# A fused two-block layer on one core: another order of the first loads, the first products and the first norm

## The reference

```python
def rmsnorm(x, g):
    xf = x.astype(jnp.float32)
    y = xf * lax.rsqrt(jnp.mean(xf * xf, axis=-1, keepdims=True) + EPS)
    return (y * g.astype(jnp.float32)).astype(x.dtype)

def gated_branch_mixer(h, w_in, ...):
    proj = h @ w_in                       # 1024 x 6144
    a_val, a_gate, u_pool, c_x, c_b, c_c, g = jnp.split(proj, PROJ_SPLITS, axis=-1)
    a = a_val * jax.nn.sigmoid(a_gate)
    a = causal_dwconv(a, conv_a_w) + conv_a_b
    ...

def first_block(x, mem, ...):
    h = rmsnorm(x, norm_mix_g[l])
    x = x + gated_branch_mixer(h, w_in[l], ...)
    x = x + memory_cross_attention(...)
    x = x + hierarchical_moe(...)
    return rmsnorm(x, norm_f_g)
```

## Time and profile before

| | us |
|---|---|
| median of 3 runs | 988.87 (988.23 to 990.27) |
| span of the profiled execution | 986.0 |
| what lies around the span, against the median | 2.9 |
| PE busy | 968.0 (98%) |
| first product | 5.89 |
| first split product (half chunk 4) | 23.62 |

### The profile page before, as it was taken

How to read it: one execution, slowest core, us unless ns; L and a number is a source line. 1 busy time by engine, 2 the same in 40 slices (tenths; PEclk the granted TensorE clock), 3 DMA queues, 4 the chain that set the end, 5 groups by cost and what they waited for, 6 DMA issues and landing times.

```text
span 986.0 us, 16667 instructions
## 1 busy us (share of the span) xinstructions
PE 968.0 (98%) x6553; PEld 888.3 (90%) x6553; DVE 749.4 (76%) x1135; ACT 518.2 (53%) x752; POOL 40.5 (4%) x42
## 2 busy tenths in 40 slices
PE   7999999999999999999999999999999999999997
PEld 6999998999999888888889999887999998999996
DVE  5699878679776886878867877965476289787876
ACT  4545533534453675777754545445465465555544
POOL 0002001000101000000001000000100120000000
PEclk9999999999999999999999999999999999999999
DMA  7945643446540677978873534221543255555541
GB/s 280 350 158 176 209 168 128 171 171 214 171 145 1 219 258 266 329 264 296 319 268 109 176 110 164 63 67 64 192 169 132 86 191 188 195 181 196 180 169 43
DMA packets 49601, 178.39 MB, mean 181 GB/s; under 512 B 5632, under 2 KB 5888, under 8 KB 49280
## 3 DMA queue, kind: packets, MB, share of 16 engines
q1 hardware_dynamic: 47952, 172.51, 51.0%
q10 hardware_dynamic: 1584, 4.99, 1.4%
HBM read 176.43 MB, written 1.05 MB: 180 GB/s over the span
## 4 chain that ended last, share of the span: by engine, by line
PE 91%; DVE 6%; DMA 1%; ACT 1%; issue 1%; DVEq 0%; SPq 0%; ACTq 0%
PE psum L715 90%; DVE wl L2169 2%; DVE work L2169 1%; DMA raw<-stream_in 1%; DVE xl L2207 1%; PE psum L953 1%; PE psum L1258 0%; DVE work L2994 0%; DVE xh L2202 0%; DVE rstd L2197 0%; DVE xT L2169 0%; ACT wh L1671 0%; DVE work L3057 0%; DVE ypair L2169 0%; ACT work L1598 0%
## 5 line engine op out<-in xcount | busy, mean ns | idle before, releaser
L1671 ACT CAST wh<-raw 128x1024 fp32r<-128x1024 f32 x292 | 303.5, 1050 | 285.3 <-PE psum L715 247.4
L2169 DVE TENSOR_TENSOR wl<-raw,wh 128x1024 fp32r<-128x1024 f32 x292 | 349.2, 1228 | 72.4 <-ACT wh L1671 69.5
L715 PE MATMUL psum<-xh,wh 128*128 128x256 f32 x976 | 275.6, 282 | 2.6 <-DVE wl L2169 2.0
L715 PE MATMUL psum<-xl,wh 128*128 128x256 f32 x976 | 272.6, 279 | 0.0
L715 PE MATMUL psum<-xh,wl 128*128 128x256 f32 x976 | 272.1, 279 | 0.0
L715 PEld LDWEIGHTS psum<-xh,wh 128*128 128x128 f32 x976 | 183.4, 188 | 5.9 <-issue 2.5
L715 PEld LDWEIGHTS psum<-xl,wh 128*128 128x128 f32 x976 | 183.5, 188 | 0.5
L715 PEld LDWEIGHTS psum<-xh,wl 128*128 128x128 f32 x976 | 183.4, 188 | 0.0
L715 PE MATMUL psum<-wh,slots 128*128 128x512 f32 x320 | 101.6, 391 | 0.0
L715 PE MATMUL psum<-memn,raw 128*128 128x256 f32 x320 | 73.3, 382 | 0.0
L715 PE MATMUL psum<-yh,wh 128*128 128x256 f32 x256 | 71.9, 281 | 0.3 <-DVE wl L2169 0.3
(11 more groups left out here) (276 smaller groups left out, 1484.9 us busy)
## 6 DMA issues: line engine op xcount, KB each, us to landing
raw<-stream_in SPq DMA_DIRECT2D x325, 512.0 KB, 4.5
memn<-mem_t_in ACTq DMA_DIRECT2D x2, 1024.0 KB, 8.6
out_rows<-work SPq DMA_DIRECT2D x4, 256.0 KB, 2.2
const<-const_in ACTq DMA_DIRECT2D x1, 581.0 KB, 3.6
xT<-x_t_in SPq DMA_DIRECT2D x2, 256.0 KB, 4.7
xT<-x_t_in ACTq DMA_DIRECT2D x2, 256.0 KB, 5.5
raw<-stream_in SPq DMA_DIRECT2D x2, 256.0 KB, 5.5
mask<-mask_in ACTq DMA_DIRECT2D x1, 512.0 KB, 13.7
```

The source lines that it names most:

```text
L715: return nc.tensor.matmul(out, w, x, start=start, stop=stop, **kw)
L1671: nc.scalar.copy(wh[:, SLOT[c], :], raw[:, c % RAW, :]).then_inc(hi_ready, 1)
L2169: return v.tensor_tensor(out, a, b, op)
```

## The change

SP now loads the four pairs of tiles of x, then half chunks 2 to 5. ACT loads, after the gains, half chunks 0 and 1 in four parts; part m has from both half chunks the 256 columns that belong to tiles 2m and 2m+1, so each transfer has two runs of 1 KB in every partition. `project_native` for unit 0 is replaced by `first_chunk`, which takes for each pair m the products of half chunks 0 and 1 and then the sum of squares of that pair. Nine products of zeros (128x512, bfloat16) stand ahead on PE. On ACT the root stands ahead of the rounding of half chunk 4. On DVE the subtraction for half chunk 4 stands ahead of the four that make `xl`, and PE's first split unit waits for `xh`, `xl` by pairs of tiles.

```diff
@@ sync: loads
-            for m in range(2):
-                q, w = slice(2 * m, 2 * m + 2), slice(HW // 2 * m, HW // 2 * (m + 1))
+            for m in range(4):
+                q = slice(2 * m, 2 * m + 2)
                 sp.dma_start(xT[:, q, :], xt_in[:, q, :]).then_inc(s_x[m], 16)
-                sp.dma_start(raw[:, 0, w], stream[0][:, w]).then_inc((s_first, landed[0])[m], 16)
-            for c in range(1, RAW):
+            for c in range(2, RAW):
                 load(c)
@@ tensor
-            def columns(out, slot, x):
+            def columns(out, slot, x, tile_pairs=None):
                 for k in range(DK):
+                    if tile_pairs and k % 2 == 0:
+                        pe.wait_ge(tile_pairs, k // 2 + 1)
...
+            def first_chunk():
+                u = units.take()
+                for m in range(4):
+                    pe.wait_ge(first_part[m], 16)
+                    for j in range(2):
+                        for k in (2 * m, 2 * m + 1):
+                            if j == 0:
+                                pe.wait_ge(xg_ready, k + 1)
+                            last = matmul(psum[:, u, j * T:(j + 1) * T], raw[:, j, k * P:(k + 1) * P], xg32[:, k, :],
+                                          k == 0 and j == 0, k == DK - 1, skip_group_check=True)
+                        if m == 3:
+                            last.then_inc(half_done, 1)
+                    pe.wait_ge(sq_folded, m + 1)
+                    last = matmul(psum[:, STAT, 0:T], ones, sq[:, 2 * m, :], m == 0, m == 3)
+                last.then_inc(stats_done, 1)
...
+            pe.wait_ge(zeroed, 2)
+            for _ in range(9):
+                matmul(psum[:, 6, :], zeros[:], zeros[:, 0:1].to_broadcast([P, 512]), True, True)
             pe.wait_ge(ones_set, 1)
-            project_native(C_WIN, xg32, xg_ready, lambda: stats(0))
+            first_chunk()
             project_native(C_WIN + 1, xg32)
-            pe.wait_ge(xn_ready, 4)
-            for n in range(C_WIN + 2, C_WIN + 16):
+            project(C_WIN + 2, xg, xn_ready)
+            for n in range(C_WIN + 3, C_WIN + 16):
                 project(n, xg)
@@ scalar
-            for m in (2, 3):
-                act.dma_start(xT[:, 2 * m:2 * m + 2, :], xt_in[:, 2 * m:2 * m + 2, :]).then_inc(s_x[m], 16)
+            for m in range(4):
+                w = slice(256 * m, 256 * (m + 1))
+                act.dma_start(raw[:, 0:2, w], stream[0:2, :, w].rearrange("h p w -> p h w")).then_inc(first_part[m], 16)
...
+            root(0)
             high.upto(4)
-            root(0)
@@ vector
                 tt(xn[:, q, :], xg32[:, q, :], two(rstd[:, 0, :]), ALU.mult).then_inc(xn_made, 1)
+            rest.upto(4)
             for m in range(4):
                 q = slice(2 * m, 2 * m + 2)
                 dve.wait_ge(xn_hi, m + 1)
```

More of the change, by code:

```diff
@@ L437, in build @@
         s_x = [sem(f"x_loaded{m}") for m in range(4)]
-        s_first = sem("first_half_chunk_loaded")
+        s_first = [sem(f"first_chunk_part{m}_loaded") for m in range(2)]
         s_mem = sem("mem_loaded")
@@ L446, in build @@
         low_ready = sem("low_ready")
+        first_part = (*s_first, landed[0], landed[1])
         half_done = sem("half_done")
@@ L741, in columns, with project @@
                 return last
-            def project(n, x):
+            def project(n, x, tile_pairs=None):
                 u = units.take()
@@ L749, in project @@
                     wait_split(c)
-                    columns(psum[:, u % UNITS, j * T:(j + 1) * T], SLOT[c], x).then_inc(half_done, 1)
+                    columns(psum[:, u % UNITS, j * T:(j + 1) * T], SLOT[c], x, None if j else tile_pairs).then_inc(half_done, 1)
             def project_rows(n, x):
@@ L998, in _, with project_native @@
             xg, yg = (xh, xl), (yh, yl)
-            def project_native(n, x, tile_ready=None, between=None):
+            def project_native(n, x):
                 u = units.take()
@@ L1005, in project_native @@
                     c = 2 * n + j
[L1006 to L1009, removed]
+                    wait_raw(c)
                     for k in range(DK):
[L1011 to L1014, removed]
                         last = matmul(psum[:, u % UNITS, j * T:(j + 1) * T], raw[:, c % RAW, k * P:(k + 1) * P],
@@ L1017, in project_native @@
                     last.then_inc(half_done, 1)
-                    if between and j == 0:
-                        between()
+            def first_chunk():
[13 more added lines that the diff above has]
+                last.then_inc(stats_done, 1)
             def native_rows(n, x, u):
```

## The result

The changed kernel is slower: 992.67 us, median of 7 runs (989.74 to 994.77), against 988.87 for the kernel before; ratio 1.0035, 95% interval 1.0024 to 1.0045. That is 3.4 us (2.4 to 4.5). The profiled execution has a span of 988.8 us against 986.0, 2.8 more; it took 990.60 us, 2.1 less than the median, so it is one of the quicker ones.

What follows compares the result with a forecast made beforehand. PE was taken as the bound (busy 968.0 of 986.0 us), the total following half chunk 6's start. Root 18.0 plus 13.7 gives 31.7 against 29.38, +2.3; 988.9 + 2.3 = 991.2 us, range 988.0 to 993.3.

Steps and rivals of the forecast that it cites:

- chain behind the root: Dependent work from root to `wl` of half chunk 6 stays 13.6 us; half chunk 6 starts 13.7 us after the root.
- main line: Late parts put the root at 18.0 and half chunk 6 at 31.7 against 29.38: +2.3 us; higher clock for all pairs.
- PE idle before pairs 1 and 2: Sign of the forecast at the head: PE waits for late parts, with pauses of 0.6 and 1.3 us.
- Rival A: Head loads: turns go by whole transfers, parts keep pace with x, root 15.4, total 988.6; chance 0.13.
- second limit: Root to `wl` of half chunk 6, before the change: 13.6 us of dependent work with only 1.0 us to spare.
- 1 KB price: Time one DMA engine spends on a 1 KB piece of ACT's parts: taken as 50 ns, between 45 and 53.
- sum of turns: Head loads: engines alternate single pieces of SP's and ACT's queues, so parts 0 to 3 land at 7.0, 9.8, 13.2, 15.3.
- 4 KB price: Time one DMA engine spends on a 4 KB piece of SP's half chunks: 161 ns.
- The clock: PE at the head: zeros from about 1.0 to 4.9 us raise the clock to the higher level (2.4 GHz) for all pairs.
- rival B: Head: parts late and PE's clock low for one pair or more, root +0.4 to +1.4, middle 992.2 us; chance 0.25.
- Stiff block: PE's work behind the head moves as one block: the total moves by what the start of half chunk 6 moves.

Runs made afterwards that it cites:

- after_again: The changed kernel measured once more with no edit: 992.40 us, ratio 1.0027 to the kernel before.
- no_zeros: The changed kernel without the nine products of zeros: 992.30 us, ratio 1.0035 to the kernel before.
- zeros_24: The changed kernel with 24 products of zeros instead of 9: 991.16 us, ratio 1.0025 to the kernel before.
- hold_sp: The changed kernel with SP issuing half chunks 2 to 5 only when part 3 has landed: 991.49 us, ratio 1.0030 to the kernel before.
- pieces_2kb: The changed kernel with half chunks 0 and 1 laid out so each part is one 2 KB run per partition: 989.84 us, ratio 1.0011 to the kernel before.
- spread_sums: The kernel before plus 12 products of zeros, root ahead of half chunk 4's cast, and each pair's sum behind its two half chunk 0 products: 986.08 us, ratio 0.9976.
- old_order: The changed kernel with root, half chunk 4's subtraction and PE's wait for `xh`, `xl` put back as before: 991.45 us, ratio 1.0033 to the kernel before.

## Why the prediction was right

*Direction and mechanism.* The direction was right, and so was the chain behind the root. Root 18.0, measured 18.34. Half chunk 4 at 24.7, measured 25.09; half chunk 6 at 31.7, measured 32.03, after a pause of 1.19 where 1.2 was forecast. From the root to the end of `wl` for half chunk 6: 13.63 us by the trace, 13.6 forecast. Parts were forecast to land at 7.0, 9.8, 13.2 and 15.3 us and landed at 7.4, 9.6, 12.7 and 15.8 (in after_again at 7.2, 9.0, 12.1 and 15.2). But why the root is late was told only by half. The main line has the late parts alone; the runs show two causes of nearly the same size:

| | part 3 landed | clock at the lower level | root |
|---|---|---|---|
| changed kernel | 15.8 | 7.7 to 11.1 | 18.34 |
| after_again | 15.2 | until 13.4 | 19.21 |
| no_zeros | 15.7 | until 11.5 | 18.29 |
| zeros_24 | 15.6 | not during the data | 18.06 |
| hold_sp | 10.7 | 8.1 to 11.6 | 17.86 |
| pieces_2kb | 11.1 | not during the data | 15.12 |

Taking away one of them moved the root by 0.3 to 0.5 us against the first profile; pieces_2kb takes away both and moved it by 3.2. So the size of the pieces is behind the loss, which the 2.6 us in the median bear out; that the root came late with part 3 is true of the first profile and not of after_again or no_zeros, where PE did not wait for it. The sign "PE idle before pairs 1 and 2" came in neither profile of the changed kernel.

Rival A is out: ACT's queue moved 1 KB packets, and the parts did not keep pace with x. The rule of the Trainium skill (DMA: Bandwidth & Descriptors, Queues, rings and completion order) by which it would hold, a switch only after a packet of some 9 to 17 descriptors, would give about two pieces of ACT's for one of SP's, since a part has 16 for each engine and x or a half chunk 8 (an estimate from that page). The trace is near this beside x (412 and 188) and not beside the half chunks (344 and 343), where the turns go by single pieces. What sets the two apart no run here shows. spread_sums shows the other side, that the second limit is met by an earlier root.

*The 1 KB price and the sum of turns.* 50 ns was taken, 45 measured; with 45 the same sum gives 15.0 for part 3, 0.8 too early. (Its 4 KB price of 161 ns is 160 by its own figures, which changes nothing.) Two things were missing in it. The last piece of x was through at 8.9 us, not at 7.0, since ACT's pieces had more than every second turn. And the sum takes all 16 DMA engines as equal: their shares of part 3 landed one after the other from 13.1 to 15.8 us, in pieces_2kb from 10.0 to 11.1. That the forecast came within 0.5 us is in part luck.

*The clock.* Here the prediction put the wrong step into its main line. It let the higher level last from the zeros on. The changed kernel's stretches, and its weight loads from 7.4 us on, say otherwise:

```profile
4.40:7.40 3.00, 0.34 (x2) 0.00 (x0) 1.53 (x5) 2.31 (x4) 0.00 (x0) 1.00 0.95 263
8.00:10.00 2.00, 2.00 (x6) 1.56 (x6) 1.59 (x5) 1.19 (x2) 0.00 (x0) 0.50 1.05 406
12.00:14.00 2.00, 2.00 (x11) 1.76 (x10) 0.00 (x0) 0.00 (x0) 0.00 (x0) 1.00 1.04 397
...
L715 PEld LDWEIGHTS psum<-kT,raw x8: 186/338/338, 7.4 to 9.9; 128*128 128x128 f32 x8
```

The clock had risen by the end of the zeros (a weight load of pair 0 still took 186 ns, the others mostly 338), fell at 7.7 us after PE's pause from 4.7 to 7.4, and was up again at 12. So rival B's mechanism was there, in this profile at a small price. Pair 0 took 3.7 us instead of 2.2, and pair 1 began at 11.1 though its part had landed at 9.6; but pair 2 would have waited until 12.7 and began at 13.3, and pair 3 did wait. In after_again, where the clock rose only at 13.4, the root came 1.2 us later than forecast, within B's +0.4 to +1.4.

*The total.* Forecast +2.3, measured +3.4 by the ratio (2.4 to 4.5), nearer to B's 992.2 than to the forecast's 991.2; after_again gave +2.7 (1.6 to 3.8). The head is 2.65 us in the first profile and 3.51 in the second. Runs carry a mean granted clock. In those with 0.998 or more, the kernel before has a median of 987.8 us (20 of 61 runs) and the changed one 990.6 (5 of 18, both groups): 2.8 apart, close to the first head. In those with 0.996 or less it is 989.2 (25 of 61) against 992.8 (10 of 18). Six of the 18 had 0.993, which no run of the kernel before, of zeros_24, of no_zeros or of pieces_2kb had (lowest 0.995). So the changed kernel seems to have a low stretch more in some runs, the one that zeros and pause make. It does not account for the rest: the first profile has this stretch, reads 0.998 and belongs to the quick runs, and no_zeros, without it, is as slow as the changed kernel. How a head of 2.65 becomes 3.4 in the median stays open.

*Stiff block.* It held in the first profile (2.64 at 33 us, 2.73 at the end). In others the slide told under old_order takes up to 0.7 us back, and each low stretch later on adds some 1.5.

*What was left out.* Rival A had the root at 15.4 with the parts on time, but the prediction did not draw from this that the sums behind 16 products are a fault of their own: in pieces_2kb the root is at 15.12, no earlier than the 14.75 of before, and with the sums in PE's pauses (spread_sums) it is at 11.45.

## What to carry to other kernels

Where two DMA queues were both full, the one with the longer contiguous runs got the larger share of the bytes by far when it had 4 KB runs against 1 KB (1.24 and 0.34 MB in 4 us). Put what is needed first into runs at least as long as what competes. When two delays lie beside each other, as the late parts and the low clock do here, taking away one shows little; count a delay as the cause only after a run without the other. When PE is moved ahead, look for the next place where it meets a chain of other engines (here 13.6 us from root to the third subtraction) and shorten the way to the start of that chain first. Products of zeros ahead of the data gave little or nothing here when a pause of 2.7 us followed them, or when PE waited for loads behind them.

## What the runs showed of the hardware

The granted clock also falls in the middle of the program, at places that differ between executions of the same code. In after_again it is 0.50 from 576.6 to 580.0 us and 1.00 around it; the same products in the kernel before ran at 1.00 throughout.

```profile
573.00:576.00 3.00, 3.00 (x27) 1.86 (x26) 2.55 (x3) 2.10 (x3) 0.00 (x0) 1.00 0.02 5
577.00:580.00 3.00, 3.00 (x16) 3.00 (x16) 2.29 (x6) 0.00 (x0) 0.00 (x0) 0.50 0.81 276
581.00:584.00 3.00, 3.00 (x25) 2.84 (x25) 0.82 (x2) 1.25 (x2) 0.00 (x0) 1.00 0.00 0
```

16 weight loads in 3 us against 25 or 26: the stretch cost 1.5 us, by the distance to the kernel before at both ends. Of the eight experiments' profiles five had such a stretch near 575 us and two near 790 (zeros_24 had both). What brings them on is open. This is more than half of the head's effect, and it makes one profiled span a poor measure of the total: pieces_2kb is 0.6 us ahead of the kernel before at half chunk 6 and 0.7 behind it at the end. Before its first change in an execution the granted clock reads 1.00 even where the durations are those of the lower level: the zeros at 2 to 4 us stood 0.43 us apart (at 0.22 in the late ones of the earlier trace rows).
